# Layer 1's expert stage: two and a half token tiles as dense products, one and a half by fetched rows

## The reference, cut to what matters

```python
q = (ht @ w_q).reshape(T, 8, 2, 64)
s = einsum('thpd,hpkd->thpk', q, sub_keys)
s_top, i_top = top_k(s, 16)
cand_s = s_top[:, :, 0, :, None] + s_top[:, :, 1, None, :]
cand_i = i_top[:, :, 0, :, None] * 128 + i_top[:, :, 1, None, :]
best_s, best_j = top_k(cand_s.reshape(T, 8, -1), 16)
experts = take_along_axis(cand_i.reshape(T, 8, -1), best_j)
gates = softmax(best_s)
a = einsum('tkd,td->tk', u_tab[experts], h)
out = einsum('tk,tkd->td', gelu(a) * gates, v_tab[experts])
```

## Time and profile before

| | us |
|---|---|
| median of three runs | 5879.87 (5877.63 to 5884.08) |
| the profiled execution's own time | 5873.12 |
| its span, first to last instruction | 5871.3 |
| granted TensorE clock, mean | 0.915 |

### The profile page before, as it was taken

How to read it: one execution, slowest core, us unless ns; L and a number is a source line. 1 busy time by engine, 2 the same in 40 slices (tenths; PEclk the granted TensorE clock), 3 DMA queues, 4 the chain that set the end, 5 groups by cost and what they waited for, 6 DMA issues and landing times. The chain is left out here.

```text
span 5871.3 us, 69786 instructions
## 1 busy us (share of the span) xinstructions
PE 4953.4 (84%) x23958; PEld 3990.8 (68%) x23958; DVE 4173.0 (71%) x7269; ACT 1841.7 (31%) x3223; POOL 857.5 (15%) x644
## 2 busy tenths in 40 slices
PE   7696737889797869999999778888885679999998
PEld 5385726633575659889888456624764569999997
DVE  1547577768635979999999767667547967676776
ACT  0222312221122753333333211131233733333333
POOL 0000005600000003333333134200000001111110
PEclk9798868999898989999999889989997789999999
DMA  6152317822122669999999467502121367777775
GB/s 225 65 165 75 111 43 274 298 65 65 54 86 90 169 181 386 396 387 400 388 395 391 157 231 269 191 26 82 51 75 52 100 215 272 276 271 277 272 276 189
DMA packets 465588, 1172.70 MB, mean 200 GB/s; under 512 B 225331, under 2 KB 259540, under 8 KB 412438
## 3 DMA queue, kind: packets, MB, share of 16 engines
q1 hardware_dynamic: 373272, 633.88, 32.0%
q0 software_dynamic: 92160, 536.91, 23.9%
HBM read 1106.46 MB, written 64.23 MB: 199 GB/s over the span
## 5 line engine op out<-in xcount | busy, mean ns | idle before, releaser
L2327 POOL DMA_INDIRECT arena<-in_peer_uv,kept x384 | 517.9, 1349 | 3622.1 <-POOLq L2212 1980.2
L232 PE MATMUL psum<-h_hi,u_ring_hi 128*128 128x384 f32 x2048 | 693.6, 339 | 18.4 <-DVE ring_lo L2415 17.9
L232 PE MATMUL psum<-h_hi,ring_lo 128*128 128x384 f32 x2048 | 694.5, 339 | 0.0
L232 PE MATMUL psum<-h_lo,u_ring_hi 128*128 128x384 f32 x2048 | 693.8, 339 | 0.0
L232 PE MATMUL psum<-v_ring_hi,w_hi 128*128 128x512 f32 x1536 | 609.6, 397 | 5.9 <-DVE ring_lo L2420 5.9
L232 PE MATMUL psum<-ring_lo,w_hi 128*128 128x512 f32 x1536 | 603.8, 393 | 0.0
L232 PE MATMUL psum<-v_ring_hi,w_lo 128*128 128x512 f32 x1536 | 600.4, 391 | 0.0
L2420 DVE TENSOR_TENSOR ring_lo<-kept,v_ring_hi 128x1024 fp32r<-128x1024 f32 x256 | 313.8, 1226 | 301.7 <-ACT v_ring_hi L2375 296.5
L2459 DVE SCALAR_TENSOR_TENSOR arena<-arena 128x1024 f32<-128x1024 f32 x384 | 482.1, 1283 | 19.2
L2447 DVE CUSTOM_DVE_ANT_0 arena<-arena 128x1024 f32<-128x1024 f32 x384 | 462.8, 1220 | 29.0 <-DMA arena<-in_peer_uv,kept 28.3
L2387 ACT ACTIVATE w_hi<-arena 128x384 fp32r<-128x384 f32 x256 | 134.7, 526 | 965.3 <-DVE arena L2430 965.3
(11 more groups left out here) (369 smaller groups left out, 10027.7 us busy)
## 6 DMA issues: line engine op xcount, KB each, us to landing
kept<-in_mix SPq DMA_DIRECT2D x312, 512.0 KB, 3.5
kept<-in_peer_u SPq DMA_DIRECT2D x256, 512.0 KB, 5.8
kept<-in_peer_uv SPq DMA_DIRECT2D x256, 512.0 KB, 4.6
kept<-in_ada SPq DMA_DIRECT2D x96, 512.0 KB, 4.4
gate_scratch<-arena SPq DMA_DIRECT2D x12, 4096.0 KB, 20.7
arena<-gate_scratch SPq DMA_DIRECT2D x128, 384.0 KB, 6.0
spec_scratch<-arena SPq DMA_DIRECT2D x4, 2048.0 KB, 8.5
arena<-in_k_dft_x SPq DMA_DIRECT2D x6, 1024.0 KB, 10.2
```

Of the source, the lines that this page charges most:

```text
L232: done = pe.matmul(out, lhs[x], rhs[y], start=first and j == 0, stop=last and j == 2)
L2327: pool.indirect_dma_start(rows[q % NBUF], None, peer_uv, bass.IndirectOffsetOnAxis(ap=row_id[q % G][:, q // G:q // G + 1], axis=0))\
```

## The change

In layer 1 (`HALVED = 1`) two and a half tiles (320 tokens) are dense, and half of tile 2 is fetched along with tile 3: tokens 256 to 319 stay dense, and come first in every dense operand; tokens 320 to 383 are fetched. A half tile of 64 tokens with 128 slots each is laid over 128 partitions with 64 slots each, so a step of the loop has one slot (even steps) or two (odd steps), 192 in all, with six row buffers in place of four.

- Selection: tile 2 has 16 chunks in place of 32, and its second store goes away. After the third pick VectorE also writes the half tile's gates and ids; SP brings them to their partitions with four small DMAs, behind a wait ahead of the last store.
- Split: the half tile's 64 tokens are copied twice side by side, turned to rows by a second set of eight transposes and copied by ScalarE; `fold`, a 128x64 matrix that adds partitions p and p+64, is made; ids and gates are interleaved with those of tile 3.
- Loop: hidden products, gelu, weighing, rounding and rest of `w`, and gate loads have 320 columns in place of 384. `w_hi` and `w_lo` become one tensor `w_parts`. The half tile's rounded weights are written twice, the second time beside their rest: its output product is then one matmul of 64 stationary columns with the rest of `v`, and one of 128 (64 rounded, 64 rest) with the rounded `v`; the two halves of the bank's partitions are added in the merge. Four matmuls in place of six.
- Merge: for tile 2 the transpose becomes two products with `fold`, one for the dense half and one for the fetched half.

Layer 0 keeps its sizes, and takes `w_parts` and the new slot indices.

```diff
-        GATHERED = {0: [("X", 3), ("C", 0)], 1: [("X", 3)]}
+        HALVED = 1
+        TD_OF = [TD if l != HALVED else TD - P // 2 for l in range(DEPTH)]
...
+                        if halved and n == dense:
+                            sp.wait_ge(half_picked.sem, half_picked.at(1))
+                            for to, x in ((half_ids_in, half_ids), (half_gates_in, half_gates)):
+                                for r in range(2):
+                                    sp.dma_start(to[64 * r:64 * r + 64, :], x[64:P, 64 * r:64 * r + 64]).then_inc(half_in.sem, 16)
                         if 0 < n <= dense:
                             store(n - 1, 0)
...
-                        if 0 < n <= dense:
+                        if 0 < n <= dense and chunks_of(n - 1) == CHUNKS:
                             store(n - 1, 1)
...
-                            for k in range(CHUNKS):
+                            for k in range(chunks_of(n - 1)):
...
+                        if halved and n == dense - 1:
+                            weights(half_gates.rearrange("p (h k) -> p h k", k=TOPK))
+                            dve.scalar_tensor_tensor(row_f, picked[:, 0, :], float(NK), picked[:, 1, :], ALU.mult, ALU.add)
+                            dve.drain()
+                            dve.tensor_scalar(half_ids, row_f, float(l * NK * P), None, ALU.add).then_inc(half_picked.sem, 1)
+                            dve.drain()
...
-        w_hi = split_tensor("w_hi", M0 + 14336, 2, TD)
-        w_lo = split_tensor("w_lo", M0 + 15104, 2, TD)
+        w_parts = split_tensor("w_parts", M0 + 14336, 2, 2 * TD)
...
+                    if not two:
+                        for r in range(2):
+                            last = dve.tensor_copy(twice[:, :, r, :], ht["X"][:, :, T:TD])
+                        last.then_inc(dve_a.sem, 1)
+                        dve.tensor_tensor(fold, ident[:, 0:P // 2], ident[:, P // 2:P], ALU.add)
+                        dve.wait_ge(half_in.sem, half_in.at(0))
+                        dve.tensor_copy(row_ids[:, :, 2], half_ids_in)
+                        dve.tensor_copy(slot_gate(l)[:, :, 2], half_gates_in)
                     dve.memset(zeros, 0.0)
-                    for g in range(len(GATHERED[l])):
+                    for g in range(2):
                         dve.memset(o_rows[g], 0.0)
...
-            NBUF = 4
+            NBUF = 6 if halved else 4
...
+                first = 3 * (k // 2) + k % 2 if halved else 2 * k
+                return range(first, first + (1 + k % 2 if halved else 2))
...
-                            last = pe_products(pe, ps[:, 6 + k % 2, 0:TD], (u_ring_hi[:, k % 2, c], ring_lo[:, k % 2, c]),
-                                               (h_hi[:, kc, :], h_lo[:, kc, :]), kc == 0, kc == KC - 1)
+                            last = pe_products(pe, ps[:, 6 + k % 2, 0:T], (u_ring_hi[:, k % 2, c], ring_lo[:, k % 2, c]),
+                                               (h_hi[:, kc, 0:T], h_lo[:, kc, 0:T]), kc == 0, kc == KC - 1)
...
+                        if halved:
+                            for half in range(2):
+                                c = slice(half * 512, half * 512 + 512)
+                                pe.matmul(ps[0:P // 2, 4 + half, :], w_parts[:, k % 2, 0:P // 2], ring_lo[:, 2 + k % 2, c],
+                                          start=False, stop=False)
+                                last = pe.matmul(ps[:, 4 + half, :], w_parts[:, k % 2, TD - P // 2:TD + P // 2], v_ring_hi[:, k % 2, c],
+                                                 start=False, stop=end)
...
-                        act.activation(w_hi[:, k % 2, :], w[:, k % 2, :], ACT.Copy).then_inc(w_rounded.sem, 1)
+                        if halved:
+                            act.activation(w_parts[:, k % 2, T:TD], w[:, k % 2, 0:P // 2], ACT.Copy)
+                        act.activation(w_parts[:, k % 2, 0:T], w[:, k % 2, 0:T], ACT.Copy).then_inc(w_rounded.sem, 1)
...
+                                if l == HALVED and t == 2:
+                                    for half, y in enumerate((x, o_rows[1])):
+                                        at = t * P + half * (P // 2)
+                                        pe.matmul(ps[:, kc, at:at + P // 2], y[:, c], fold, start=True, stop=True)
+                                else:
+                                    last = pe.transpose(ps[:, kc, t * P:(t + 1) * P], x[:, c], ident)
```

More of the change, by code:

```diff
@@ L2001, in hots @@
                         if t == dense - 1:
-                            first, end = (min(CHUNKS, -(-3 * n // 2)) for n in (first, end))
+                            first, end = (min(chunks_of(t), -(-3 * n * chunks_of(t) // (2 * CHUNKS))) for n in (first, end))
                         for n in range(first, end):
@@ L2136, in stage_select @@
             consts_in.add(16)
-            for c in gate_stored:
-                c.add(16 * dense)
+            chunks = sum(chunks_of(t) for t in range(dense))
+            for half, c in enumerate(gate_stored):
+                c.add(16 * (dense - (1 if halved and half else 0)))
+            if halved:
+                half_picked.add(1)
+                half_in.add(64)
             pe_a.add(2 * nt)
-            pe_b.add(CHUNKS * dense)
+            pe_b.add(chunks)
             pe_c.add(dense)
@@ L2143, in stage_select @@
             scores_kept.add(2 * nt)
-            act_b.add(CHUNKS * dense)
-            weighted.add(CHUNKS * dense)
-            equal_ready.add(CHUNKS * dense)
+            act_b.add(chunks)
+            weighted.add(chunks)
+            equal_ready.add(chunks)
             turned.add(dense)
@@ L2209, in stage_split @@
         def stage_split(l):
-            two = len(GATHERED[l]) == 2
+            two = l != HALVED
+            T = TD_OF[l]
+            twice = area(M0 + 4096, KC, 2, P // 2)
             with nc.Block() as block:
@@ L2236, in _ @@
                     last.then_inc(pe_a.sem, 1)
+                    if not two:
+                        pe.wait_ge(dve_a.sem, dve_a.at(1))
+                        for kc in range(KC):
+                            last = pe.transpose(ps[:, 2 + kc // 4, (kc % 4) * P:(kc % 4 + 1) * P],
+                                                twice[:, kc].rearrange("p a b -> p (a b)"), ident)
+                        last.then_inc(pe_a.sem, 1)
                 @block.vector
@@ L2457, in add_rows @@
                         dve.drain()
[L2458 to L2462 removed]
+                        for g, q in enumerate(slots_of(k)):
+                            dve.scalar_tensor_tensor(o_rows[g], rows[q % NBUF][:, D:2 * D], slot_w[:, q:q + 1], o_rows[g], ALU.mult, ALU.add)\
+                               .then_inc(rows_free.sem, 1)
@@ L2463, in step @@
+                    def step(b, k, at):
                         if at_most(b, k, NK - 1):
```

133 lines of the change are left out of this document (79 added, 54 removed).

## The result

The changed kernel takes 5832.91 us (median of four runs, 5822.62 to 5836.66), the kernel before 5878.75 on the same chips: a ratio of 0.9924 with a 95% interval of 0.9907 to 0.9940. It is faster, by 46 us and not by 151; the range began at 5714 and ended at 5785, so the time lies above it. The profiled execution's span is 5834.9 us, 36.4 less than before.

A forecast was written before the change was run, and what follows sets the result against it. TensorE alone was taken to bound layer 1's expert loop. Loop -147, jitter +8, loop start +3, selection -18.1, split +2.6 and merge +0.5 sum to -151 us: from 5879.9 to 5729 us, range 5714 to 5785.

The forecast's parts named there:

- What bounds the kernel, and TensorE's new step: Layer 1's expert loop: TensorE alone bounds it, and its step falls from 8.37 to 7.22 us, 147 us in all.
- The narrow operand at zero: Half tile's output product: four changes of shape a step from 64-column matmuls cost nothing; upper figure 0.09 us each, 46 us.
- Rival 2: Layer 1's output products: the narrow operand costs up to 0.09 us at each change of shape, 5775 us; chance 0.08.
- rival 4: Layer 1's loop: TensorE drains at each of four changes of shape, 0.35 us each, slower at 5908 us; chance 0.03.
- Rival 3: Hidden products: fewer columns don't shorten them because 188 ns loads bind; only 0.46 us a step won, 5817 us; chance 0.04.
- Selection, split, merge: Stages around layer 1's loop: selection 18.1 us shorter, split 2.6 us longer, merge 0.5 us longer.
- Start of the loop: Start of layer 1's loop: six gathers in place of four delay u's load, 3 us more, once.
- VectorE: Layer 1's loop: VectorE is busy 6.96 us a step, 96% of TensorE's 7.22, so it still fits.
- the cover behind the dot products: Layer 1's loop: VectorE's two remainders, 1.6 us, cover ScalarE's gelus and rounding of v, 1.7; could cost 0.1 a step.
- DMA: Layer 1's loop: 2.79 MB a step takes 7.09 us, 98% of 7.22; u's load fits by under 1 us; jitter 0.06.
- The alternation of one and two slots: VectorE in layer 1's loop: always three slot halves between one remainder of v and the next, so no pile-up.
- Rival 1: Layer 1's loop: the feed (DMA, or VectorE and ScalarE with waits) binds at 7.45 to 7.8 us, 5751 to 5795; chance 0.22.

The follow-up runs named there:

- the early version: The changed kernel with layer 1's rests of u and v in memory of their own and their loads released after VectorE's split: 5709.94 us, ratio 0.9720.
- the kernel without the third slots: The changed kernel with every third slot of layer 1 neither fetched nor computed: 5733.69 us.
- the six products: The early version with the half tile's output product as six matmuls of 64 stationary columns in place of four: 5763.94 us, ratio 0.9804.
- u and v alone: Two runs of the early version, each with one wait changed back: only u's loads released early, 5796.13 us; only v's, 5735.82 us.

## Why the prediction was wrong

- *What bounds the kernel, and TensorE's new step*: right. 24 hidden pitches of 0.147 us and 16 of 0.23 give 7.22; the early version runs 7.16, the kernel without the third slots 7.26. In the changed kernel itself undisturbed products have these pitches.
- *The narrow operand at zero*: right, by the same steps and by the 54 us of the six products. Rival 2 is out, and with it rival 4. Rival 3 is out by the pitch.
- *Selection, split, merge*: -17.7, +1.9 and +1.5 against -18.1, +2.6 and +0.5. The terms stand. *Start of the loop*: the first weighing comes 20.4 us after the first rounding of u, against 20.9 before, so the 3 us for two more gathers didn't come.
- *VectorE*: busy 191.5/200 x 7.16 = 6.86 us a step in the early version, against 6.96. Right. So was the 0.1 us a step for the cover behind the dot products: VectorE waits 9.8 us in 97 steps there for the rounding of v.
- *DMA*: this is the step that failed. The prediction said "It fits by under 1 us", for u's load alone, with layer 0's landing of 7.5 us for every block, and gave 0.06 us a step for jitter. u by itself nearly fits: a late u stands before two of 33 stalls. The chain of v was never priced. The load of its block k+1 is released by output product k-1, and through the fixed orders of ScalarE and VectorE hidden product k+4 hangs on it. Between the two TensorE has two hidden and two output products, 2 x (3.53 + 3.69) = 14.4 us in place of 16.7 before. Into that must go 0.3 us to the issue, the landing and, for an even block, 8.4 us from v's rounding to the product. This leaves 5.7 us for a landing that took 8.5 in the median. Shortening the products shortens this allowance as much as it shortens two steps.
- An estimate of the stall from this: the mean landing of the even blocks, 8.2 us, is 2.5 too long. A stall two steps earlier gives the next load as much more time, so half remains, 1.25 us in every two steps. Measured are 48.0 us in some 43 pairs of steps, 1.1 us. TensorE's 7.2 us, 0.55 for half of that stall and 0.2 for the clock leave 0.1 of the 8.09, for the ends of matmuls and the shorter waits. The simpler sum on which the expectations for u and v alone were built (issue, landing, rounding, rest and output product, 15.0 us for two steps) gives 7.5 us and falls short of it.
- *The alternation of one and two slots* "doesn't pile up" in VectorE's busy time, as said, but it does in the chain: the late v is the one behind which two accumulations stand, 2.48 us. The throughput of the rings, on which the 98% was worked out, was never the limit (388 GB/s in the early version).
- *Rival 1* named the place, "the VectorE and ScalarE chain with its waits", but priced it by the rings' rate and not by a landing time in the chain: its 7.45 to 7.8 us a step was too low (and the middle of its 5751 to 5795 is 5773, not 5768). Its far bound, 7.93 us from 351 GB/s at full share, came near to the 8.09 by chance: that rate was a result of the waits and not their cause. The sign of being wrong that the prediction gave, idle time before hidden products released by the remainder of u, is what the profile shows.
- *The clock* was missing altogether: with stalls of up to 2.1 us TensorE's products behind them ran partly at 1.2 GHz, an estimated 0.2 us a step.

## What to carry to other kernels

When the engine that bounds a loop gets faster, check for each load the time from when its buffer comes free to when its data is needed, and follow it through whatever stands behind it in the fixed orders of the other engines; that allowance shrinks with the step, while here the landing time grew with the traffic that the change added. Price the late landings and not the median. If a buffer is held longer than its data is read (here by a result written over it), separating the two can be worth more than the work that was saved: 123 us against 46.

## What was not expected of the hardware

A single pause of 1.9 us between matmuls, in a stream that was dense on both sides, was followed by a stretch at the lower clock (pitch 0.263 us for 0.147), and so were 16 of 23 pauses of 1.8 to 2.1 us. A 512 KB load landed in 4.2 to 5.0 us in the median at a DMA share of 0.78, and in 7.9 (u) and 8.5 (v) at 0.92 in every second block, in 4.4 and 5.4 in the others: the late landings came up to twice as late well before the rings were full. That the rhythm of one and two gathers makes the difference is argued, not shown; without every third gather v's even and odd blocks land in 5.2 and 5.3 us.

A load of 64 stationary columns takes 134 ns instead of 188, and its matmul no less time:

```profile
L2427 PEld LDWEIGHTS psum<-ring_lo,w_parts 128*64 128x64 f32 x220 | 29.4, 134 | 9.6
```
